# First half reordered: low parts of the in projection on GpSimd, layer norm beside its last units, gate products in PSUM, three attention units begun at once

## What is computed

```
h = rmsnorm(x) ; z = h @ w_in                       # "in": 36 units of 128 output columns
a = a_val * sigmoid(a_gt)
a = silu(layernorm(dwconv31(a) + bias))  ; y_a = a @ w_a_out     # "a_out"
s = sc_b * dwconv3(sc_c * sc_v)          ; y_b = s @ w_b_out     # "b_out"
x = x + (g_a*y_a + g_b*y_b) @ w_o                                # "o"
x = x + ffn(rmsnorm(x))                                          # "up", "down"
x = x + sigmoid(rmsnorm(x) @ w_ple_gate) * (p @ w_ple)           # "gate", "ple"
x = rmsnorm(x) ; then block 2: rmsnorm, projection to q, k, v    # norm "final", "in2"
... attention, out2, up2, down2 (unchanged)
```

## Time and profile before

| | |
|---|---|
| median of 3 runs | 823.68 us (821.07, 823.68, 823.71) |
| the profiled execution's own time | 822.88 us |
| its span, first to last instruction | 821.1 us |
| busy: PE, PEld | 779.7 us, 748.8 us |
| busy: DVE, ACT, POOL | 600.5 us, 449.6 us, 264.9 us |
| mean granted TensorE clock | 0.984 |

### The profile page before, as it was taken

The page is one execution under the profiler, slowest core; times in us unless marked ns, Lnnn a source line. Parts: engine busy times, 40 slices in busy tenths (PEclk is TensorE's granted clock), DMA queues, the critical chain, the costliest instruction groups (busy, mean ns, idle before and its releaser), DMA issues.

```text
span 821.1 us, 16957 instructions
## 1 busy us (share of the span) xinstructions
PE 779.7 (95%) x5954; PEld 748.8 (91%) x5954; DVE 600.5 (73%) x1058; ACT 449.6 (55%) x756; POOL 264.9 (32%) x160
## 2 busy tenths in 40 slices
PE   5989899899999999999899999699999999999996
PEld 5889899899999999999899998699999999988885
DVE  5899976767888888434957686479999999973333
ACT  7444354556565655444655564586666666653431
POOL 0366644464122212345563011642112221222220
PEclk9999999899999999999989999989999999999999
DMA  8445454455555557545433332525555555565551
GB/s 281 141 155 179 161 192 130 133 181 181 191 180 190 180 198 247 178 148 167 135 122 111 104 103 79 179 84 175 181 182 184 188 181 179 204 203 187 181 173 51
DMA packets 37771, 135.44 MB, mean 165 GB/s; under 512 B 4448, under 2 KB 4704, under 8 KB 37728
## 3 DMA queue, kind: packets, MB, share of 16 engines
q1 hardware_dynamic: 37728, 134.86, 49.7%
HBM read 133.80 MB, written 1.05 MB: 164 GB/s over the span
## 4 chain that ended last, share of the span: by engine, by line
PE 52%; DVE 3%; POOL 2%; issue 1%; ACT 1%; DVEq 0%; ACTq 0%; POOLq 0%
PE bank L1618 13%; PE bank L1619 12%; PE bank L1620 12%; PE bank L1948 4%; PE bank L1950 4%; PE bank L1949 4%; POOL sumsq L540 1%; PE bank L1823 1%; PE bank L1822 1%; DVE tmp L1382 1%; POOL X L658 1%; PE bank L1832 1%; DVE w_lo L1024 1%; PE bank L1640 0%; PE bank L1848 0%
## 5 line engine op out<-in xcount | busy, mean ns | idle before, releaser
L1618 PE MATMUL bank<-h_hi,w_hi 128*128 128x256 f32 x1424 | 410.7, 288 | 22.1 <-DVE h_lo L1036 13.4
L1619 PE MATMUL bank<-h_lo,w_hi 128*128 128x256 f32 x1424 | 406.4, 285 | 0.0
L1620 PE MATMUL bank<-h_hi,w_lo 128*128 128x256 f32 x1424 | 406.2, 285 | 0.0
L527 POOL TENSOR_TENSOR w_lo<-raw,w_hi 128x1024 fp32r<-128x1024 f32 (+2 forms) x78 | 192.9, 2477 | 407.4 <-ACT w_hi L684 407.4
L684 ACT ACTIVATE w_hi<-raw 128x1024 fp32r<-128x1024 f32 (+2 forms) x246 | 261.9, 1067 | 87.5 <-PE bank L1950 43.2
L1618 PEld LDWEIGHTS bank<-h_hi,w_hi 128*128 128x128 f32 x1424 | 276.7, 194 | 29.2 <-issue 21.3
L1024 DVE TENSOR_TENSOR w_lo<-raw,w_hi 128x1024 fp32r<-128x1024 f32 (+1 forms) x168 | 218.6, 1302 | 109.8 <-ACT w_hi L684 109.7
L1619 PEld LDWEIGHTS bank<-h_lo,w_hi 128*128 128x128 f32 x1424 | 277.1, 195 | 0.0
L1620 PEld LDWEIGHTS bank<-h_hi,w_lo 128*128 128x128 f32 x1424 | 276.8, 194 | 0.0
L1064 DVE TENSOR_TENSOR bank<-bank,scales 128x256 f32<-128x256 f32 x124 | 53.1, 431 | 37.3 <-PE bank L1620 29.5
L1291 DVE TENSOR_TENSOR f_lo<-src,f_hi 128x256 f32 (+1 forms) x54 | 58.7, 1086 | 0.5 <-ACT f_hi L831 0.5
(11 more groups left out here) (198 smaller groups left out, 924.3 us busy)
## 6 DMA issues: line engine op xcount, KB each, us to landing
raw<-in_w_up SPq DMA_DIRECT2D x108, 512.0 KB, 3.3
raw<-in_w_in SPq DMA_DIRECT2D x54, 512.0 KB, 3.4
raw<-in_w_down SPq DMA_DIRECT2D x32, 512.0 KB, 4.3
raw<-in_w_down SPq DMA_DIRECT2D x16, 704.0 KB, 4.1
raw<-in_w_o SPq DMA_DIRECT2D x8, 512.0 KB, 3.4
raw<-in_w_gate SPq DMA_DIRECT2D x8, 512.0 KB, 3.6
raw<-in_w_out SPq DMA_DIRECT2D x8, 512.0 KB, 3.4
raw<-in_w_b_out SPq DMA_DIRECT2D x4, 512.0 KB, 3.3
```

The source lines that it names most:

```text
L527: nc.gpsimd.tensor_tensor(w_lo[s][:, 0:n], raw[s][:, 0:n], w_hi[s][:, 0:n].bitcast(f32), ALU.subtract).then_inc(lo_ready[s], 1)
L1618: nc.tensor.matmul(ps, wh, hi[:, k, :], start=start and n == 0, stop=False)
L1619: nc.tensor.matmul(ps, wh, lo[:, k, :], start=False, stop=False)
L1620: last = nc.tensor.matmul(ps, wl, hi[:, k, :], start=False, stop=stop and n == len(ks) - 1)
```

## The change

1. `on_pool`: in the in projection POOL makes the low parts of units 5 and 7 to 31; DVE those of 0 to 4, 6, 32 to 35 and of all units of b_out, a_out, ple and o, half of which POOL made.
2. `CONV_STEPS`: from unit 20 on four steps a unit until they are used up (by unit 28), in place of three and later two.
3. The mean of the layer norm is taken before unit 32 of the in projection, its statistics after unit 33, its broadcast after unit 34. These were after b_out 0, 1 and 2. DVE's subtractions and ACT's squares move with them. The unit loop on PE is written out from unit 32.
4. Order of phases b_out, a_out, ple instead of b_out, ple, a_out. All four `gate_branch` come after the layer norm's chain.
5. X is loaded by four DMAs that ACT issues, ahead of its table load, not by SP behind the first weight unit; SP's second unit is issued right after its first.
6. PE runs 8 float32 matmuls of 128x128 on constants, once the first weight unit has landed, before its first product.
7. Gate units: the sigmoid and the product with `branch` are written in place in PSUM; the bank is free when X has been added.
8. in2: `first_units` begins three units (six chunks of each, then two of each); the statistics come after all three, the broadcast after unit 3.
9. Norm "final": DVE makes the quotient in four small instructions, POOL one power on four columns and one product.

```diff
-    ("in", 36, 8), ("b_out", 4, 8), ("ple", 4, 4), ("a_out", 4, 8), ("o", 8, 8),
+    ("in", 36, 8), ("b_out", 4, 8), ("a_out", 4, 8), ("ple", 4, 4), ("o", 8, 8),
...
+IN_STATIC = 32
+WARM_UP = 8
...
 CONV_STEPS = [{5: 1, 6: 2, 7: 3}.get(u, 0) if u < 8 else (2 if u % 3 < 2 else 1) if u < 20 else
-              3 if u < 24 else 2 for u in range(36)]
+              4 if u < 29 else 0 for u in range(36)]
...
-    if u < UNIT0["b_out"]:
-        return 4 <= u and (u % 2 == 1 or u % RING == 0 and u > IN_DEFERRED)
     if u < UNIT0["up"]:
-        return u % 2 == 1 or u == UNIT0["a_out"]
+        return RING < u < IN_STATIC and u != 6
...
-        r[TILE0["gate"] + c] = ("pg_ready", c + 1)
+        r[TILE0["gate"] + c] = ("sq_src", SQ_SRC0["final"] + c + 1)
...
-            for n in range(4):
-                load_x(n)
...
+            for n in range(4):
+                act.dma_start(X[:, 2 * n:2 * n + 2, :], d["x"].rearrange("p (c t) -> p c t", c=DC)
+                              [:, 2 * n:2 * n + 2, :]).then_inc(x_in[n], 16)
             act.wait_ge(memset_done, 1)
...
+                if u == IN_STATIC:
+                    for k in range(CK):
+                        act.wait_ge(ln_step, k + 1)
+                        square("ln", k, conv[:, k, :])
...
-                if c >= 4:
-                    act.wait_ge(res_step, c - 4 + 1)
-                nc.scalar.activation(ev[c % 4][:], bank[slot(TILE0["gate"] + c)][:, 0:TOK],
-                                     ACT.Sigmoid).then_inc(pg_ready, 1)
+                tile = bank[slot(TILE0["gate"] + c)][:, 0:TOK]
+                nc.scalar.activation(tile, tile, ACT.Sigmoid).then_inc(pg_ready, 1)
...
+                if 20 + n == IN_STATIC:
+                    dve.wait_ge(mean_ready, 1)
+                    for c in range(CK):
+                        nc.vector.tensor_tensor(conv[:, c, :], conv[:, c, :], rbc[:, 0:TOK],
+                                                ALU.subtract).then_inc(ln_step, 1)
+                if 20 + n == IN_STATIC + 2:
+                    mean_square("ln")
...
+            pe.wait_ge(memset_done, 2)
+            pe.wait_ge(raw_in[0], 16)
+            for n in range(WARM_UP):
+                nc.tensor.matmul(rbc[:, 0:P], ones_over[:, 0:P], ones_over[:, 0:P],
+                                 start=True, stop=True)
...
-            with pe.Fori(0, 3, 1) as it:
+            with pe.Fori(0, (IN_STATIC - 24) // RING, 1) as it:
...
+            pe.wait_ge(conv_step, 4 * TAPS_A)
+            for c in range(CK):
+                last = nc.tensor.matmul(rbc[:, 0:TOK], ones_over[:, 0:P], conv[:, c, :],
+                                        start=c == 0, stop=c == CK - 1)
+            last.then_inc(mean_ready, 1)
+            for u in range(IN_STATIC, UNIT0["b_out"]):
...
+                if u == IN_STATIC + 1:
+                    mean_squares("ln")
+                if u == IN_STATIC + 2:
+                    broadcast_rsqrt("ln")
...
-                    first_pair("in2", h2_hi, h2_lo, deferred_ready("in2"), norm="final")
-                elif n > 1 and step["unit"] is not None:
+                    first_units("in2", 3, h2_hi, h2_lo, deferred_ready("in2"))
+                elif n > 2 and step["unit"] is not None:
                     project(step["unit"])
+                if n == 2:
+                    mean_squares("final")
+                if n == 3:
+                    broadcast_rsqrt("final")
```

More of the change, by code:

```diff
@@ L60, in unit_blocks @@
             return blocks
-TILE0 = {"in": 0, "b_out": 36, "ple": 40, "a_out": 44, "o": 48, "up": 56, "down": 100,
+TILE0 = {"in": 0, "b_out": 36, "a_out": 40, "ple": 44, "o": 48, "up": 56, "down": 100,
          "gate": 108, "in2": 116}
@@ L403, in build @@
         ms_ready = sem("ms_ready")
+        ms_step = sem("ms_step")
         pow_step = sem("pow_step")
@@ L779, in _ @@
                                      bias=vcol("b_gate", b)).then_inc(gates_ready, 1)
-            for i in range(4):
-                ahead(UNIT0["b_out"] + i)
-                if i == 0:
-                    for c in range(CK):
-                        act.wait_ge(ln_step, c + 1)
-                        square("ln", c, conv[:, c, :])
+                if u == IN_STATIC:
+                    for k in range(CK):
+                        act.wait_ge(ln_step, k + 1)
+                        square("ln", k, conv[:, k, :])
             def keep_embedding(i):
@@ L822, in _ @@
                     round_chunk(CHUNK0["mix"] + c, h2_hi[:, c, :])
+            for i in range(4):
+                ahead(UNIT0["ple"] + i)
+                keep_embedding(i)
             for c in range(DC):
@@ L1244, in _ @@
             affine(2)
+            ahead(UNIT0["b_out"])
             scale_chunk(3)
@@ L1253, in _ @@
             for i in range(4):
-                ahead(UNIT0["ple"] + i)
+                if i > 0:
+                    ahead(UNIT0["b_out"] + i)
+                gate_branch(i)
             for i in range(4):
@@ L1670, in plain_units, with first_units @@
                         broadcast_rsqrt(norm)
-            def first_pair(name, hi, lo, ready, norm=None, late=2):
+            def first_units(name, count, hi, lo, ready, norm=None, late=2):
                 u, t = UNIT0[name], TILE0[name]
                 for first, end in ((0, DC - late), (DC - late, DC)):
-                    for n in range(2):
+                    for n in range(count):
                         if first == 0:
@@ L1713, in _ @@
                              True, True).then_inc(unit_done, 1)
+            pe.wait_ge(conv_step, 4 * TAPS_A)
[4 more added lines that the diff above has]
+            for u in range(IN_STATIC, UNIT0["b_out"]):
+                unit_here(u)
+                bank_free(u)
+                products(bank[slot(u)][:, 0:TOK], slot(u), 0, range(DC), h_hi, h_lo, True, True
+                         ).then_inc(unit_done, 1)
+                if u == IN_STATIC + 1:
+                    mean_squares("ln")
+                if u == IN_STATIC + 2:
+                    broadcast_rsqrt("ln")
             def paired_units(name, i, k, hi, lo, ready):
@@ L1755, in up_units @@
                              ).then_inc(unit_done, 1)
-            first_pair("up", h_hi, h_lo, deferred_ready("up"), norm="up")
+            first_units("up", 2, h_hi, h_lo, deferred_ready("up"), norm="up")
             for n in (2, 3):
@@ L1791, in project @@
                 bank_free(t)
[L1792 to L1799 removed]
+                products(bank[slot(t)][:, 0:TOK], slot(UNIT0["in2"] + u), 0, range(DC),
+                         h2_hi, h2_lo, True, True).then_inc(unit_done, 1)
             def transpose_v(i):
```

105 lines of the change are left out of this document (29 added, 76 removed).

## The result

| | before | after |
|---|---|---|
| median, ten runs each, taken side by side | 822.34 us | 826.22 us |
| the profiled execution's own time | 822.88 us | 826.23 us |
| its span | 821.1 us | 824.4 us |
| mean granted TensorE clock | 0.984 | 0.986 |

The ratio is 1.0042 with a 95% interval of 1.003 to 1.0055. That is under the 0.5% set as "same", and 826.2 lies inside the range of 811 to 828, but the forecast was 822.0: a small gain was expected and a small loss came, 4 us from the number. The profiled span moved by +3.3 us where -1.5 was forecast, so 4.8 us are to be explained.

What follows compares the result with a forecast made beforehand. PE, busy 95% of the span, was taken as the bound, except units 8 to 31, DVE's. -3.0 up to o and +1.5 in gate and in2 give -1.5 on 822.88: 821.4, as median 822.2, stated as 822.0; range 811 to 828.

Steps and rivals of the forecast that it cites:

- The start: Up to unit 1: warm-up and X from a second issuer gain 1.0 us; bounds 2.2 gained to 0.5 lost.
- Units 8 to 31: In projection: POOL's three low parts in a row hold DVE's taps, period 10.1 us; unit 23 at 87.7, +1.1 us.
- The mean: Ahead of unit 32: taps ready at 117.4, PE still about 4 us, clock loss 2.5; b_out 0 at 131.4 before that loss.
- b_out to o: From b_out 0 to o: norm chain hidden, 0.8 us wait for ple 2's low part; o at 162.5, -3.0 us in all.
- In o a unit's low part and one addition leave DVE inside PE's 2.88 us; nothing else changes up to the gate units: From o to the gate units: no further change, so the -3.0 us reached at o stays.
- Gate and in2: Gate to v's transposes: shorter chunk wait, but 2.9 us wait for the third low part, 2.5 clock loss, uncovered broadcast: +1.5 us.
- The second clock loss: In in2: a further clock loss, upper bound +4 us for that stage; among other slower cases with chance 0.04.
- A: Units 8 to 31: successor taps slip in before POOL's next low part, period is PE's; 817.7 us, chance 0.22.
- B: in2: the third unit's low part is in time and the clock holds there; 816.6 us, chance 0.15.
- C: Units 8 to 31: the second successor tap also waits for a whole low part, 2.5 us a group; 829.5 us, chance 0.15.

Runs made afterwards that it cites:

- e1: Kernel after with X's four DMAs issued by SP behind the first weight unit, warm-up kept: 824.09 us, ratio 1.0011 to the kernel before.
- e2: Kernel after without the eight warm-up matmuls: 826.52 us, ratio 1.0040 to the kernel before.
- e10: e9 without the warm-up matmuls: 810.07 us, ratio 0.9852 to the kernel before.
- e8: Kernel after with the edits of e1, e3 and e4 together: 815.89 us, ratio 0.9920 to the kernel before.
- e3: Kernel after with the low parts of odd units of o made by POOL: 823.47 us, ratio 1.0012 to the kernel before.
- e4: Kernel after with in2 in the old order (two units first, broadcast in the middle of unit 3): 820.00 us, ratio 0.9962 to the kernel before.
- e5: Kernel after with only in2's broadcast moved back into the middle of unit 3, three units still begun: 823.20 us, ratio 1.0004 to the kernel before.
- e6: Kernel after with mean, statistics and broadcast one unit later, POOL making low parts up to unit 33: 820.20 us, ratio 0.9978 to the kernel before.
- e7: Kernel after with the low parts of units 13, 16, 19 and 22 on DVE again: 826.31 us, ratio 1.0048 to the kernel before.
- e11: Kernel after with the in projection's low parts divided as in the kernel before: 830.23 us, ratio 1.0097 to the kernel before.
- e9: e8 plus the later mean of e6: 810.43 us, ratio 0.9856 to the kernel before.

## Why the prediction was off, step by step

**The start (-1.0; measured +1.6): wrong, and the first step that failed.** The bound "at worst X or unit 0 lands later by the 0.5 us that one issue takes" took the delay from the issue. What counts is the bytes that move beside the first weight unit: 0.60 MB of X and some 0.3 MB of units 1 and 2 by the time it was there, and with X back behind it, and units 1 and 2 behind X, it came 2.45 us earlier (e1). The rule of the Trainium skill cited there (DMA: Bandwidth & Descriptors, section "Issuing engines are not separate DMA queues") says that the transfers of all issuers share the engines and interleave. The trace agrees with that (0.60 MB of ACT's and 0.81 MB of SP's moved by 7.05 us), and read as a statement on landing and not on issue time alone it would have given the sign. The warm-up's 3.1 us was measured at 3.75 and its value at 0 (e2, e10).

**Units 8 to 31 (+1.1): the mechanism was right, its size too large.** Three low parts in a row on POOL (7.19 us; forecast 7.35), the first tap and one of its successors held (1.33 us, and 3.03 for the two), a period of 9.93 us for 10.1. Unit 23 at 87.94 contains the late start of 1.6 us, which nothing absorbed: it is at 86.28 in e8, where X is SP's and unit 3 starts at 20.59, as before the change. Without the late start unit 23 comes 0.4 us earlier than before the change, not 1.1 later. Where a first miss hid behind a second, the number of 87.7 looked right.

**The mean: right.** Taps ready 117.5 (117.4), a wait of 3.5 us (about 4), half clock from 118.36 on. PE loses 1.7 us by it, and not 2.5: 3.4 us at half clock. b_out 0 at 133.88 equals the 131.4 of the text with its 2.5 of clock loss on top, but partly by luck: the taps come 0.2 later, the clock costs 1.7, and the mean's and the norm's matmuls take 0.6 more than forecast. All these forecasts leave out the start's -1.0, as unit 23's did.

**b_out to o: right.** The chain is hidden, no wait for `mix`, ple 2 waits 1.04 us (0.8), and the stage takes 29.58 us (28.8 + 0.8). o came 1.0 us later than forecast: the start is 2.6 us worse, the groups are 1.4 better, and 0.2 are won in the mean and behind it.

**"In o a unit's low part and one addition leave DVE inside PE's 2.88 us; nothing else changes up to the gate units": wrong.** DVE's work of a unit is 2.1 us (1.23, 0.41 and 0.48), inside 2.88, but it is one link of a circle with ACT of 3.38 us. 1.5 us of the gain were lost there (e3).

**Gate and in2 (+1.5; measured +1.0): right in kind in each part.** L1361 takes 0.42 us and L1382 took up to 2.3; chunk 5's wait is 0.8 us (0.2), the third low part is ready at 411.5 (411.8), the wait 2.4 (2.9), the clock falls at 411.91 and costs 1.7 us (2.5), the broadcast is uncovered. e4 shows that this order costs 5.4 us against the old one.

**The second clock loss: named only as a bound, and the largest single term, 3.0 us.** It came behind the stop of 2.0 us before v's transposes; cutting that stop to 0.5 us ended it (e5), though half of the 3.0 us is missing in five other kernels with the same stop. The forecast had this stop in its 1.9 us of scales and copies, and put a clock loss behind the longer stop only.

In sum: 2.6 (start) - 1.6 (groups, mean and what follows up to o) + 1.5 (o) - 0.2 (up to in2) - 0.5 (in2) + 3.0 (attention) = 4.8, which is what lies between -1.5 and +3.3. Of the rivals, A (DVE keeps ahead) fell with the taps held in each group; B fell with the wait of 2.4 us; C, which has the right sign, fell too, as only one of the two successors is held. The loss came from what stood beside C at a chance of 0.04 (an X that lands late, a second clock loss) and from o, which no rival had.

What stays open: why the same stop of 2.4 us for the third unit's low part was followed by half clock in the kernel after, e1, e2, e5 and e6, and not in e3, e7 and e11; and why PE's stop of 3.5 us at the mean was followed by 3.4 us of half clock in five of the kernels, by 6.8 in e2 and e4, and by none in e7. The code alone doesn't decide it: the traced execution of e7 had a mean granted clock of 0.990 and took 823.24 us, the other five 0.983 to 0.986 and 825.66 to 826.73. A stretch of 3.4 us costs PE 1.7 us, so two traces that differ by that much need not differ in what was edited.

## What to carry to other kernels

Before a transfer is given to a second issuer, ask which bytes then move ahead of or beside the first one that everything waits for. Look for the circle before counting an engine's load: two engines that were each idle for 1.4 to 1.6 of 3.38 us set the pace of o, as one's next step waited for the other's last. And where an operation of one engine is on PE's path only at one point, moving that point by one unit of PE's work can win what its wait costs with no engine made faster (4.6 us up to b_out 0 in e6).

## What the runs showed of the hardware

In the rows shown DVE was held by POOL only where its instruction reads SBUF alone: a low part on DVE takes 1.23 us beside a still POOL and 2.40 (e7) to 3.12 (e11) beside a busy one, two short taps take 1.00 and 3.03 us, and in e7 the hold moved from the taps to the low part that DVE makes ahead of them. The 31-tap convolution's instructions, with one operand in PSUM, run at 0.40 to 0.41 us beside POOL. Transfers of two issuers moved side by side, and the first 512 KB weight unit came 2.45 us later when 0.9 MB of other transfers had moved beside it than when 0.13 MB had (e1). And a stop of 2.0 us ahead of v's transposes was followed by the 1.2 GHz level in every kernel that had it (the kernel after, e1, e2, e3, e6, e7, e11), a stop of 0.5 us at the same place in none (the kernel before, e4, e5, e8, e9, e10): e5, with nearly the same waiting in all (2.1 and 2.2 us), cut in two, is 3.0 us shorter.
